# Nine slots in place of seven for the expert weights of a four-layer network kernel, two of them borrowed from a position bias and from norm weights

## The reference

```python
def swiglu(x, w1, w3, w2):
    return (jax.nn.silu(x @ w1) * (x @ w3)) @ w2

def moe_ffn(x, router_w, w1, w3, w2):
    ...
    logits = (xt @ router_w).astype(F32)
    top_v, top_i = lax.top_k(logits, TOP_K)
    top_w = jax.nn.softmax(top_v, axis=-1)
    gates = jnp.sum(jax.nn.one_hot(top_i, N_EXPERTS, dtype=F32) * top_w[..., None], axis=1)
    y = jnp.zeros_like(xt)
    for e in range(N_EXPERTS):
        y = y + gates[:, e:e + 1].astype(x.dtype) * swiglu(xt, w1[e], w3[e], w2[e])
```

## Time and profile before

| | |
|---|---|
| median of 3 runs | 2364.59 us (2361.65 to 2365.38) |
| profiled execution, its own time | 2356.97 us |
| its span | 2355.2 us |
| PE busy | 2300.1 us, 98% |
| PE weight loads | 1890.5 us, 80% |
| DVE busy | 1812.8 us, 77% |
| ACT busy | 1392.4 us, 59% |
| moved by DMA | 582.10 MB, mean 247 GB/s |

### The profile page before, as it was taken

One profiled execution on the slowest core, in us unless ns is written; L12 is line 12 of the kernel. 1 busy time (PEld: TensorE's weight loads), 2 busy tenths in 40 slices (PEclk: granted clock), 3 DMA queues, 4 the chain that ended last, 5 costly groups with the idle time before them and its releaser, 6 DMA issues.

```text
span 2355.2 us, 29291 instructions
## 1 busy us (share of the span) xinstructions
PE 2300.1 (98%) x11179; PEld 1890.5 (80%) x11179; DVE 1812.8 (77%) x2343; ACT 1392.4 (59%) x1588; POOL 31.7 (1%) x44
## 2 busy tenths in 40 slices
PE   8999999999999999999999998999999999999998
PEld 7788887887778887788778776888888888888887
DVE  5964568898875558998999898899775669987655
ACT  4444534677855447877887785565544545654543
POOL 0000000000000000000000000000000000000000
PEclk9999999999999999999999999999999999999999
DMA  8376543799976579999999995654565665455663
GB/s 283 106 223 188 183 156 100 298 362 359 396 281 215 196 238 368 402 397 373 395 404 380 370 402 223 196 160 143 170 199 187 185 210 162 121 175 168 201 187 125
DMA packets 212557, 582.10 MB, mean 247 GB/s; under 512 B 17228, under 2 KB 26584, under 8 KB 212281
## 3 DMA queue, kind: packets, MB, share of 16 engines
q1 hardware_dynamic: 210108, 571.87, 69.9%
q0 software_dynamic: 1872, 6.82, 0.8%
q10 hardware_dynamic: 428, 1.45, 0.2%
HBM read 579.02 MB, written 1.07 MB: 246 GB/s over the span
## 4 chain that ended last, share of the span: by engine, by line
PE 80%; DVE 9%; DMA 5%; ACT 4%; issue 1%; ACTq 0%; POOL 0%; SPq 0%; POOLq 0%; DVEq 0%
PE tile L895 21%; PE tile L897 21%; PE tile L896 21%; PE aux L1018 4%; DMA units<-in_moe_w 3%; DVE units_parts L2499 3%; PE aux L1362 2%; PE tile L1476 2%; PE tile L1477 2%; ACT high L1887 1%; DVE nat_parts L2499 1%; DVE k_buf_parts L2499 1%; PE tile L1374 1%; PE tile L1376 1%; DVE q_buf_parts L2499 1%
## 5 line engine op out<-in xcount | busy, mean ns | idle before, releaser
L2499 DVE TENSOR_TENSOR units_parts<-units,high 128x1024 fp32r<-128x1024 f32 (+3 forms) x357 | 523.9, 1485 | 108.3 <-ACT high L1887 105.8
L1887 ACT ACTIVATE high<-units 128x1024 fp32r<-128x1024 f32 (+3 forms) x357 | 448.0, 1273 | 184.4 <-PE tile L897 59.5
L896 PE MATMUL tile<-units_parts,acts 128*128 128x512 f32 (+2 forms) x1392 | 533.1, 383 | 0.0
L895 PE MATMUL tile<-high,acts 128*128 128x512 f32 (+2 forms) x1012 | 401.2, 396 | 6.2 <-DVE units_parts L2499 3.6
L897 PE MATMUL tile<-high,acts 128*128 128x512 f32 (+2 forms) x1012 | 389.7, 385 | 0.0
L896 PEld LDWEIGHTS tile<-units_parts,acts 128*128 128x128 f32 x1392 | 262.9, 189 | 47.9 <-issue 1.0
L895 PEld LDWEIGHTS tile<-high,acts 128*128 128x128 f32 x1012 | 191.3, 189 | 44.4 <-DVE units_parts L2499 5.7
L897 PEld LDWEIGHTS tile<-high,acts 128*128 128x128 f32 x1012 | 191.0, 189 | 38.7
L896 PE MATMUL tile<-units_parts,zbuf_parts 128*128 128x512 f32 x456 | 177.4, 389 | 0.0
L897 PE MATMUL tile<-high,zbuf_parts 128*128 128x512 f32 x368 | 143.3, 389 | 0.0
L2499 DVE TENSOR_TENSOR units_parts<-units,gbuf_parts 128x2048 fp32r<-128x2048 f32 x48 | 109.9, 2290 | 17.0 <-ACT gbuf_parts L1887 16.8
(11 more groups left out here) (527 smaller groups left out, 4869.1 us busy)
## 6 DMA issues: line engine op xcount, KB each, us to landing
units<-in_moe_w SPq DMA_DIRECT2D x192, 1024.0 KB, 7.2
units<-in_w_in SPq DMA_DIRECT2D x134, 512.0 KB, 3.8
units<-in_w_ff SPq DMA_DIRECT2D x128, 512.0 KB, 3.7
q_buf<-in_moe_w SPq DMA_DIRECT2D x48, 1024.0 KB, 7.7
k_buf<-in_moe_w SPq DMA_DIRECT2D x48, 1024.0 KB, 8.1
nat<-in_moe_w SPq DMA_DIRECT2D x48, 1024.0 KB, 7.3
units<-in_ffn_w SPq DMA_DIRECT2D x48, 512.0 KB, 4.2
units<-in_w_out SPq DMA_DIRECT2D x32, 512.0 KB, 3.6
```

Source lines behind the costliest of these rows:

```text
L895: nc.tensor.matmul(bank, lhs[0], high, start=start, stop=False)
L896: nc.tensor.matmul(bank, lhs[0], low, start=False, stop=False)
L1887: nc.scalar.activation(high_slot(SG[0], n) if wide_ else high_slot(SG[0], n)[:, 0:cols], halves(weights) if wide_ else weights[:, 0:cols], ...
L2499: V.tensor_tensor(low, weights, high, ALU.subtract).then_inc(SG[0].low_ready, 1)
```

## The change

The expert units get two more slots: slot 7 is `bias2`, slot 8 the first two rows of `gain`. Which slot a unit takes and how many units must be done before its load now comes from a `Ring` named `EXPERTS`. Eight slots are always open; `gain` is open for units 0 to 83 with the floor 1, and again from unit 129 ((2 + 1) x 42 + 1 + 2) to unit 272 with the floor 129. `bias2` is stored to DRAM before the second layer's w_out loads and loaded back in block 2, behind the small parameters of its first layer. POOL's wait before it loads norm weights becomes `GAIN_FREE`, the last unit in `gain` plus one, 265.

```diff
-EXPERT_COLS, EXPERT_UNITS, EXPERT_HIGHS = 2048, 7, 4
+EXPERT_COLS, EXPERT_UNITS, EXPERT_HIGHS = 2048, 9, 4
+EXPERT_OWN = 7
...
-assert MOE_UNITS % EXPERT_UNITS == 0
+assert MOE_UNITS % EXPERT_OWN == 0
+GAIN_LENT = [(0, LARGE * MOE_UNITS, 1),
+             ((LARGE + 1) * MOE_UNITS + TURN_AFTER + 2, (N_EXP - 2) * MOE_UNITS + MOE_UNITS // 2,
+              (LARGE + 1) * MOE_UNITS + TURN_AFTER + 2)]
+EXPERTS = Ring(ROUNDS * MOE_UNITS, (EXPERT_OWN + 1) * [[(0, ROUNDS * MOE_UNITS, 0)]] + [GAIN_LENT])
+GAIN_FREE = 1 + EXPERTS.last[EXPERT_OWN + 1]
...
-        bias2 = sb("bias2", [P, NSA_H, SEQ])
+        bias2, bias2_parts = shared("bias2", [P, NSA_H, SEQ])
...
+        expert_ring += [bias2[:, :, :].rearrange("p h t -> p (h t)"), gain[:, 0:2, :].rearrange("p i n -> p (i n)")]
+        expert_lows += [bias2_parts[:, :, :].rearrange("p h t -> p (h t)"),
+                        gain_parts[:, 0:2, :].rearrange("p i n -> p (i n)")]
...
+        bias_kept = nc.dram_tensor("bias_kept", (P, NSA_H, SEQ), F32)
...
-                k = m % EXPERT_UNITS
-                return expert_ring[k], expert_lows[k], expert_loaded[k], m // EXPERT_UNITS + 1
+                k = EXPERTS.slot[m]
+                return expert_ring[k], expert_lows[k], expert_loaded[k], EXPERTS.loads[m]
...
-                shared_ = lent[m - 3] if 3 <= m < EXPERT_UNITS else 0
-                return max(n - EXPERT_UNITS + 1, shared_)
+                if m < EXPERT_OWN:
+                    return lent[m - 3] if m >= 3 else 0
+                return len(STREAM1) + EXPERTS.free[m]
...
+                if expert_unit(sig_, n) == EXPERT_OWN:
+                    sp.wait_ge(bias2_stored, 16)
...
+                    sp.wait_ge(S.unit_done, FF1_AT)
+                    sp.dma_start(bias_kept.ap(), bias2[:, :, :]).then_inc(bias2_stored, 16)
                     wide(S, A["w_out"][l], 0, D - P)
...
                         load_params2(l)
+                        if l == 0:
+                            sp.dma_start(bias2[:, :, :], bias_kept.ap()).then_inc(bias2_loaded, 16)
...
-                    pool.wait_ge(S.unit_done, len(STREAM1) + (LARGE + 2) * MOE_UNITS)
+                    pool.wait_ge(S.unit_done, len(STREAM1) + GAIN_FREE)
...
                 bank = aux_in()
+                dve.wait_ge(bias2_loaded, 16)
```

More of the change, by code:

```diff
@@ L586, in build @@
         bias_loaded = sem("bias_loaded")
+        bias2_stored = sem("bias2_stored")
+        bias2_loaded = sem("bias2_loaded")
         nat_ready = sem("nat_ready")
```

## The result

The changed kernel takes 2368.62 us (median of 20 runs, 2361.23 to 2371.14) against 2362.86 us before (median of 20 runs, 2356.54 to 2365.96). The ratio is 1.0018, with a 95% interval from 1.0010 to 1.0025: on 2362.86 us that is 4.3 us slower, from 2.4 to 5.9 (the two medians lie 5.8 us apart). The forecast was 8.9 us slower. The sign was right and the measured time lies in the range, but the size is about half of what was forecast, and 4.3 us lies within the 0.2% (4.7 us) that I had called hard to tell from no change, a case to which I gave only 0.12.

A forecast was written before the change was run, and what follows sets the result against it. PE was taken as the floor, with odd expert rounds bound by DMA once stock ran out. Slots saving 5.2 us and the bubble costing 14.1 gave +8.9 us on the 2364.59 us median: 2373.5 us, range 2365 to 2381.

The forecast's parts named there:

- What bounds the kernel: Expert rounds: PE paces even rounds; odd rounds use up stored units, then run at DMA's 2.63 us a unit.
- The bubble at unit 129: Round 3: the load of unit 129 waits for unit 128's end, stock runs out, costing 14.1 us.
- What more slots give: Rounds 1, 5, 6 and 7: two more slots of stock save about 5.2 us, from 0 to 25.9.
- the distance between folds: Matmul batches every eight units: 21.09 us (round 1) and 20.55 (round 5) against 19.9 with stock; gives back 1.2 and 0.65.
- That two slots give the stock of two: Start of rounds 1 and 5: two more slots hold 5.3 us more of DMA work; round 7 gets one more.
- Store and reload, and GpSimd's load, at nothing: Bias store near 348 us, reload in block 2, norm weights moved to round 6: all hidden, cost nothing.
- (a): Odd rounds: depth gives nothing since VectorE holds them; +14.1 us, 2378.7 us; chance 0.11.
- (b): Rounds 1, 5 and 7: slots pay for the bubble, 11.8 us less, 2352.8 us; decides from 14.1 saved; chance 0.06.
- (c): Rest of round 3 catches up as DMA exceeds 398 GB/s; swallowed whole, -5.2 us, 2359.4 us; chance 0.06.
- (d): Round 3: idle PE gets a lower clock, units take 3.6 us, +5 us more, 2378.5 us; chance 0.09.
- (e): Bias store or reload is not hidden: 2.6 to 8.8 us more, 2376 to 2382 us; chance 0.05.
- The signs that I had named: Right: round 3 123 to 124 us, PE idle some 9; wrong: round 3 under 119, rounds 1 and 5 at 104 or less.

The follow-up runs named there:

- e7_mid: Changed kernel with the norm-weight slot (gain) reopened at unit 133 instead of 129, same wait for unit 128's end: 2356.59 us against 2359.90 before, ratio 0.9980.
- e1_late: Changed kernel with the norm-weight slot (gain) reopened at unit 138 instead of 129: 2347.71 us against 2363.04 before, ratio 0.9942.
- e2_bubble: Kernel before, seven slots, with only the load of unit 129 made to wait for unit 128's end: 2378.72 us, ratio 1.0069 against before.
- e3_eight: Changed kernel with only the bias slot as eighth, gain not lent, GpSimd's norm-weight load at its old place: 2352.23 us, ratio 0.9953 against before.
- e4_keep: Kernel before, seven slots, with only the position bias's store to DRAM and reload added: 2362.94 us against 2363.04 before, ratio 1.0004.
- e5_pool: Kernel before, seven slots, with only GpSimd's wait before its norm-weight loads moved from unit 168 to 265: 2363.26 us against 2359.90, ratio 1.0011.

## Why the prediction was right and wrong

**What bounds the kernel: right.** Even rounds hold at PE's pace in every kernel with seven slots or more, to within 2 us; odd rounds lived on stock and then on DMA. The 2.63 us a unit held too: from unit 130 to unit 167 the changed kernel's landings are 2.61 us apart on the mean, most of them 2.56, four 2.7 and one 3.7. By the Trainium skill, page "DMA: Bandwidth & Descriptors", section on the anatomy of one DMA, the bytes alone take their number over 436 GB/s, which makes an estimate of 2.4 us for such a unit. That section describes transfers issued by GpSimd, and these come from SP's queue: their usual distance, 2.56 us, is 6% longer, and the measurement is what the sums go by.

**The bubble at unit 129: right in place and mechanism, and in size with some luck.** Forecast +14.1 us in round 3, measured +14.1. The last landing was forecast 105.2 us after unit 128's end and came after 104.3, so it moved by 13.2 us and not by 14.1. The rest is a term that the sum had at nothing: from the last split's start to the round's end it is 7.4 us (997.51 to 1004.9) where it was 6.4 before (981.17 to 987.6). The two errors cancel. "DMA is the bound from there to the round's end" is borne out by e7_mid, where the debt is paid with hardly a standstill. What I had not seen is that 14.1 is a balance: the wait costs 17.0 us and takes from round 3 the 2.9 us that depth gives there (e1_late). e2_bubble gives the same round 3 with seven slots.

**What more slots give: the step that failed.** The term was 5.2 us, and the rounds show 8.5: 3.0, 1.3, 2.7, 0.1 and 1.4 us in rounds 1, 4, 5, 6 and 7, for 3.0, 0, 1.15, 0.4 and 0.7. The working gave the distance between folds its 1.2 and 0.65 us and then said: "I put 0.5 us on what each of the three still holds". That was the mis-sized term: the stretch from the third fold to the round's end held 1.8, 1.95 and 1.4 us. In rounds 5 and 7 it accounts for 2.2 us of the 3.3 us that the term is short, and round 4, put at 0, for 1.3; round 6 takes 0.3 off. The 3.0 us of round 1 is right by luck: 1.3 of it was to bring its tail down to that of round 5, but the two tails differ as before (41.8 against 40.4 us, 43.6 against 42.35 before); both grew shorter by about as much. A better bound could be had from the rows than the 8.9, 7.4 and 9.6 us of VectorE idle: 16 units follow the third fold, and at the distance of folds with stock at hand (19.9 / 8 us a unit) they take 39.8 us, 3.8, 2.55 and 1.6 us under the tails of before. That would have been 7.9 us where 5.15 were found, too much this time; the tails of rounds 1 and 5 also hold the gathering, and those two stay above 39.8 (41.8 and 40.4). Round 4 was put at 0 because PE bounds it. Depth gives 1.1 to 1.4 us there (e3_eight, e1_late, e7_mid), and in the changed kernel 1.0 us of it stands at the first three units of the round. That their loads came late out of round 3 is the likely reason; no run tests it by itself.

**That two slots give the stock of two: wrong.** The eighth slot gives all, and the ninth, whose return carries the stall, nothing that a round shows (e3_eight against e1_late). With eight slots ScalarE waits for landings for 2.7 to 3.4 us in rounds 1, 3 and 5 (9.0 in round 5 before), and taking that away too doesn't shorten the round. What then holds an odd round, at 103.6 to 107.2 us with VectorE busy for 96 to 99 of it and PE for 101 to 105, no run tests. The other way the curve is steep: seven slots in place of six are worth about 32 us, eight in place of seven about 11, nine in place of eight from nothing to a few microseconds.

**Store and reload, and GpSimd's load, at nothing: not contradicted.** e4_keep gives +0.9 us with an interval that holds 0; e5_pool gives 0 to +5 us, where rounds 6 and 7 of a kernel with seven slots are 1.6 us longer.

**The rivals.** (a), depth gives nothing: excluded by rounds 1 and 5. (b), savings pay for the bubble: the savings were 8.5, short of the 14.1 from which it decides. (c), the bubble is swallowed: excluded by round 3. (d), the clock falls in the bubble: it did, and no cost of it shows. The window of the changed kernel over the stall and the rest of the round after it:

```profile
894.00:908.00 14.00, 5.32 (x17) 4.32 (x18) 7.29 (x7) 7.56 (x5) 0.00 (x0) 0.63 0.99 380
...
904.00:1004.90 100.90, 94.91 (x460) 74.08 (x459) 93.97 (x62) 87.54 (x85) 0.00 (x0) 0.98 1.03 407
```

The granted clock is 0.63 from 894 to 908 us, so for most of the time at 1.2 GHz in place of 2.4: it fell while PE stood idle for 9.5 us and was still low in PE's first 4 us of work. But landings set the end of the round, and those PE could follow: from the last split's start to the round's end it is 7.4 us here and 7.4 us in e7_mid (987.76 to 995.2), where the clock stayed at 1.00. (e): no sign, within what e4_keep can tell.

**The signs that I had named.** Round 3 at 124.0 us, rounds 1 and 5 less by 3.0 and 2.7, PE idle for 9.5 us and splits behind landings to the end of round 3 came as said. Round 4 was to be the same and was 1.3 us shorter. And 103.6 us in round 5 met half of what I had called a sign of being wrong, "rounds 1 and 5 at 104 or less": the savings were larger than the sum had them.

**The chances.** The parts named add to 0.80 and 0.11, not 0.79 and 0.12. 0.79 on slower by over 0.2% took the size of the bubble as certain and the savings as small. With the tails read from the fold distance, as above, the savings would have been about 10.2 us and the sum about +3.9, on the other side of the 4.7 us that I took as the line to no change.

The rounds of the changed kernel add to +5.6 us, the stretch behind them +0.5; the timed runs say +4.3, 2.4 to 5.9. That agrees within what one profiled execution of each kernel can tell.

## What to carry to other kernels

A wait placed in a queue of loads, ahead of a stretch that is bound by transfers, costs a little less than one transfer for each load that the queue is behind when the wait ends (here 17.0 us for seven loads and 6.7 us for three, where a transfer takes 2.6), even if the engines hardly stand still; a buffer that is lent and taken back should come back at a unit whose floor has long passed (138 in place of 129 turned 4 us lost into 14 us won). Count what another buffer gives up to the end of the stretch and not only where stock is first used up, and try it with one buffer before two: the eighth slot gave all that the rounds show, by itself 11 us, and needed no return. A sum of a gain and a loss that nearly cancel deserves wide chances, however well each mechanism is understood.

## What the runs showed that I had not expected

- The round with the stall is as long with seven slots as with nine (124.1 and 124.0 us).
- Depth is worth 32 and 11 us for the seventh and eighth slot, and for the ninth nothing that a round shows. A slot also keeps the transfers going: with six slots the rate falls to 294 GB/s late in round 5, with eight it holds 385 and more from the eighth slice on.
- PE's granted clock of 0.63 over 14 us in the middle of a round left no trace in the round's length, where transfers bound what followed. In round 2, which PE bounds, a mean of 0.91 over 18 us goes with 1.6 us more.
